# The couplings of a scan step moved into the last level of the step before

## The reference, cut to what matters

```python
def wkv_scan(r, w, k, v, a, b, S0, reverse):
    def step(S, inp):
        rt, wt, kt, vt, at, bt = inp
        sa = jnp.einsum('bhvk,bhk->bhv', S, at)
        S = S * wt[:, :, None, :] + sa[..., None] * bt[:, :, None, :] + vt[..., None] * kt[:, :, None, :]
        return S, jnp.einsum('bhvk,bhk->bhv', S, rt)
...
    for d in range(2):
...
        s_fin, yd = wkv_scan(rh, decay, kd, vh, -kk, kk * a, S0[d], reverse=(d == 1))
```

## Time and profile before

| | us |
|---|---|
| median of 3 runs | 2342.22 |
| lowest, highest | 2335.45, 2346.71 |
| the profiled execution | 2353.76 |
| its span, first to last instruction | 2352.0 |
| mean granted TensorE clock in it | 0.92 |
| first scan | 429 to 609 |
| second scan | 1611 to 1811 |

### The profile page before, as it was taken

One profiled execution on the slowest core, in us unless ns is written; L12 is line 12 of the kernel. 1 busy time (PEld: TensorE's weight loads), 2 busy tenths in 40 slices (PEclk: granted clock), 3 DMA queues, 4 the chain that ended last, 5 costly groups with the idle time before them and its releaser, 6 DMA issues. The chain is left out here.

```text
span 2352.0 us, 49452 instructions
## 1 busy us (share of the span) xinstructions
PE 2112.7 (90%) x21626; PEld 1341.5 (57%) x21626; DVE 682.5 (29%) x1672; ACT 540.6 (23%) x1260; POOL 266.3 (11%) x461
## 2 busy tenths in 40 slices
PE   6999999799899999999999599998998999987784
PEld 2454444688544444445556465556997787744442
DVE  1033334766331011210010214455465311200001
ACT  2123322455320001201111223323354301110011
POOL 0000000444000001101111200002333000011111
PEclk8999989889999999999999799996579999999897
DMA  7148717000122122539999711110000345799993
GB/s 286 69 155 345 294 37 253 3 4 4 55 90 107 54 92 96 223 111 390 397 397 389 275 37 51 61 50 2 3 3 8 151 149 190 271 382 400 393 403 118
DMA packets 55811, 399.64 MB, mean 170 GB/s; under 512 B 6672, under 2 KB 22928, under 8 KB 33648
## 3 DMA queue, kind: packets, MB, share of 16 engines
q1 hardware_dynamic: 43440, 361.94, 40.1%
q0 software_dynamic: 8576, 23.08, 2.6%
q10 hardware_dynamic: 3648, 12.45, 1.7%
HBM read 365.47 MB, written 31.98 MB: 169 GB/s over the span
## 5 line engine op out<-in xcount | busy, mean ns | idle before, releaser
L535 PE MATMUL ps<-H,memory 128*128 128x512 f32 (+2 forms) x1728 | 615.9, 513 | 8.8 <-DMA memory<-in_w_in 7.0
L535 PEld LDWEIGHTS ps<-H,memory 128*128 128x128 f32 (+1 forms) x1728 | 328.3, 191 | 284.9 <-issue 251.5
L1080 PE MATMUL ps<-memory 128*32 128x256 f32 x5120 | 302.1, 398 | 46.6 <-DMA memory<-in_eu 45.1
L535 PE MATMUL ps<-memory 128*128 128x512 f32 (+3 forms) x928 | 320.3, 496 | 6.7 <-issue 3.0
L1080 PEld LDWEIGHTS ps<-memory 128*32 128x32 f32 x5120 | 179.8, 115 | 164.9 <-issue 71.1
L535 PEld LDWEIGHTS ps<-memory 128*128 128x128 f32 (+1 forms) x928 | 173.9, 188 | 144.9 <-issue 127.5
L889 PE MATMUL ps<-memory 64*64 64x32 f32 x5120 | 223.1, 244 | 17.9 <-POOL memory L2042 6.9
L889 PEld LDWEIGHTS ps<-memory 64*64 64x64 f32 x5120 | 209.4, 164 | 28.5 <-POOL memory L2042 10.2
L1105 PE MATMUL ps<-memory 128*32 128x256 f32 x2560 | 144.8, 380 | 4.9 <-ACT memory L1468 3.8
L2042 POOL TENSOR_TENSOR memory<-memory,cons 128x256 f32<-128x256 f32 x160 | 113.2, 728 | 100.4 <-DVE memory L1725 78.8
L1105 PEld LDWEIGHTS ps<-memory 128*32 128x32 f32 x2560 | 80.0, 110 | 59.5 <-ACT memory L1468 10.1
(11 more groups left out here) (268 smaller groups left out, 2019.0 us busy)
## 6 DMA issues: line engine op xcount, KB each, us to landing
memory<-in_eg SPq DMA_DIRECT2D x32, 2048.0 KB, 16.6
memory<-in_eu SPq DMA_DIRECT2D x32, 2048.0 KB, 21.9
memory<-in_ed SPq DMA_DIRECT2D x32, 2048.0 KB, 22.8
memory<-in_w_ada SPq DMA_DIRECT2D x24, 2048.0 KB, 9.4
memory<-in_w_in SPq DMA_DIRECT2D x20, 2048.0 KB, 7.4
expert_rows<-memory SPq DMA_DIRECT2D x4, 3456.0 KB, 23.7
memory<-in_w_out SPq DMA_DIRECT2D x4, 2048.0 KB, 8.2
memory<-expert_rows ACTq DMA_DIRECT2D x19, 384.0 KB, 10.3
```

The source lines that it names most:

```text
L535: ins = mm(ps[0:M, bank, 0:w], lhs(k), rhs(k), start=(k == 0), stop=(k == n - 1))
L1080: ins = mm(out_.rearrange("p (x n) -> p x n", x=2), XGT[:, k, g * GROUP:g * GROUP + GROUP], sets[b][:, 0:2, k * 512 + c * P:k * 512 + c * ...
```

## The change

`couple(k + 1)` is issued in the last level of step k, between the join of side 1 and the two growths, instead of in step k + 1 between values and grams 1; `couple(0)` is issued ahead of the loop, before `grams(0, 0)`. A step then begins with grams 0, values, grams 1. The wait of the couplings for the last `inverse` of the step before becomes one for its first half level (`halved(N - 1, 1, d)`: the addition of level 0), which stands for the reading of the couplings' banks by VectorE. In the last level of the last step none is issued.

```diff
                     for d in both:
                         pe.wait_ge(sem("keys"), nth(N, d))
                         if N:
-                            pe.wait_ge(sem("inverse"), inverses(N - 1, 5, d))
+                            pe.wait_ge(sem("inverse"), halved(N - 1, 1, d))
...
+                couple(0)
                 for k in range(STEPS):
                     grams(k, 0)
                     if k:
                         values(k - 1)
-                    couple(k)
                     grams(k, 1)
                     for n in range(len(LEVELS)):
                         join(k, n, 0)
...
                         join(k, n, 1)
                         if k and n == 0:
                             correct_values(k - 1)
+                        if n == 4 and k + 1 < STEPS:
+                            couple(k + 1)
                         grow(k, n, 0)
                         grow(k, n, 1)
```

## The result

| | before | after |
|---|---|---|
| median, us | 2340.73 (10 runs, 2331.74 to 2352.43) | 2320.41 (10 runs, 2309.27 to 2328.78) |
| ratio, 95% interval | | 0.9905 (0.988 to 0.993) |
| the profiled execution, us (span) | 2353.76 (2352.0) | 2325.34 (2323.6) |

What follows compares the result with a forecast made beforehand. TensorE was taken to bound the scan at both clocks, leaving only its idle time to win: 4.3 + 1.7 + 0.4 + 0.7 - 0.4 - 0.65 - 0.85 = 5.2 us, so 2342.2 - 5.2 = 2337.0 us, range 2324 to 2352.

Steps and rivals of the forecast that it cites:

- The gaps: Scan: TensorE's idle time at step starts closes, 5.2 us less in sum; chance of this forecast 0.46.
- a wait before the couplings in both steps 0: Last level of step 0, each layer: couplings wait for VectorE's late keys, costing 0.65 and 0.85 us.
- A start at full clock: Step starts at full clock: first join's idle 0.46 to 0.41, second's 0.57 gone; 0.62 us each, seven starts, 4.3 us.
- A step at low clock: Four starts at low clock: no gap to close, gain 0; second layer's steps still 28.8 to 29 us.
- Starts behind two reads: Starts at 517 and 538, where grams 0 waits for GpSimd's queries: gain 0.84 each, 1.7 us for both.
- The beginning of the first scan: First layer: couplings run while grams 0 waits for GpSimd's queries; about 0.7 us won at the first join.
- The beginning of the second scan: Second layer: couplings want both keys where grams 0 waits for the first alone; 0.4 us lost.
- The clock: Low-clock spells inside steps: about 5.3 us each; forecast took spells as often as before, give or take one.
- rival 3: Step starts: the dense block loses the couplings, rises are missed at 11.4 us each; 2371.4 or 2359.8 us; chance 0.12.
- My own last sign of being wrong: Profile after: another number of low-clock steps, which would carry the result whatever the gaps did.
- Rival 2: Full-clock steps: less idle at starts prevents two clock falls, 10.6 us besides the 5.2; 2338.0 or 2326.4; chance 0.24.
- Rival 1: Step starts: ScalarE's later copies make the second join's gap reappear before the growth; about 2354 us; chance 0.18.

Runs made afterwards that it cites:

- e1: Changed kernel with the couplings issued behind the last level's two growths, directly ahead of grams 0: 2334.84 us, 0.997 of the kernel before.
- e3: Kernel before with the couplings moved early everywhere except in the second layer's four narrow steps: 2331.71 us, 0.9962 of the kernel before.
- e2: Kernel before with the couplings moved early only for the second layer's four narrow steps: 2332.88 us, 0.9956 of the kernel before.
- e9: Changed kernel with three extra one-column copies on ScalarE ahead of each step's values copies: 2317.37 us, run once.
- e10: Kernel before with three extra one-column copies on ScalarE ahead of each step's values copies: 2347.06 us, run once.
- e5: Changed kernel with the couplings of steps 2 and 3 of the second layer directly behind the update: 2318.56 us, 0.9908 of the kernel before.
- e6: The changed kernel itself, measured again with nothing altered: 2318.88 us, 0.991 of the kernel before.
- e4: Kernel before with only the couplings' wait weakened to the first half level, their place unchanged: 2338.04 us, 0.9986 of the kernel before.
- e8: Kernel before with the grams of the four narrow steps made full width, couplings at the old place: 2325.98 us, 0.9928 of the kernel before.

## Why the prediction was wrong, point by point

**The gaps (sum 5.2 us): right in mechanism, too small.** What I named came: the coupling matrix behind the last addition, the second join's wait gone, the first join waiting for ScalarE, the wait on the queries gone, a wait before the couplings in both steps 0 (0.65 and 0.85 us said, 0.7 and 0.84 found). The terms that were mis-sized:

- A start at full clock: 0.62 us said, 0.93 found. The first join's wait was to be 0.41 and is 0.58, since ScalarE starts its copies 0.27 us behind the start of grams 1, where I had 0.12. The gain I left out is larger: I took the 32 couplings at the same price in both places, and they cost 0.72 us between values and grams 1 and 0.38 in the last level. Seven starts: 2.2 us more than said.
- A step at low clock: unchanged, I said, 28.8 to 29. It is 28.4. The weight loads at such a start, after, answering to the earlier trace rows:

```profile
1653.51 1.78 PEld L805 LDWEIGHTS ps<-memory 64*128 64x128 f32 x16
1655.06 0.66 PEld L788 LDWEIGHTS ps<-cons,memory 64*128 64x128 f32 x8
1655.59 1.83 PEld L805 LDWEIGHTS ps<-memory 64*128 64x128 f32 x16
```

  From values to grams 1 it is 0.53 us here and was 1.83 in the step of the earlier trace rows (values at 1666.15, grams at 1667.98): 1.30 less, for 0.85 more between the last level's join of side 1 and grams 0.
- Starts behind two reads: 0.84 each said, 1.01 and 0.97 found (from the last level's join of side 1 to the first growth 7.71 and 7.62 us before, 6.70 and 6.65 after).
- The beginning of the first scan: 0.7 said, 0.8 found. From the end of the keys to the first join it was 5.74 us and is 4.92 (418.69 to 423.61). The second join of step 0, which waited 0.42 us, waits no more; I had left that out.
- The beginning of the second scan: 0.4 lost said, 0.24 found (from the end of the keys to the first join 4.68 us, now 4.92). With the wait before the couplings its step 0, at 0.50 in both traces, takes 0.7 us more (24.50 to 25.20).

By these the idle time comes to about 9 us: the 5.2, 2.2 for the starts, 0.4 for each of two low-clock steps and about 1 for the last three lines. The split over the runs gives 9.4, with e1 at 7.2 and e3 at 7.8. They agree as far as runs can tell.

**The clock: the step that failed.** My sum has no term for the clock. I let the number of spells vary by one or two inside full-clock steps, at 5.3 us each, and took the 123 us spell of the earlier trace rows as fixed, because TensorE was busy 99% in it and being busier could not end it. That being busy isn't enough stood in the rows; that nothing else could end the spell didn't follow. What I didn't ask is what TensorE was busy *with*. Where I weighed the couplings' new neighbours (rival 3), I counted what grams lose and took what readout and update gain as an offset, at a rise near 560 in the first scan, and never looked at the second layer, whose steps have narrow grams and no readout. There the update is the one block of products over all 128 partitions at a step's end (128*64 in its row, against 64*64 of a join), and the couplings now stand beside it. That carries about 12 of the 21 us. My own last sign of being wrong, another number of low-clock steps, is what came.

**Rival 2 (fewer spells, 2326.4 on the median's level, chance 0.24)** named the right kind and nearly the right size, at the wrong place and for the wrong reason. It had idle gaps at starts cause falls. e3 closes the gaps of every wide step and moves no low clock (342 against 340 us), and e1 closes them all and moves none. e2 leaves the wide steps as they were and moves 33 of the 44 us. So closed gaps aren't what raised the clock.

**Rival 1** fell: TensorE's waits on ScalarE's copies of the joins come to 3.0 us in the first scan, and were 2.9 before. In the second they rose from 2.6 to 4.4, since its narrow steps now run in part at full clock, where such waits show. In part it holds for the step itself: the wait of a start did change its name, from GpSimd's mask to ScalarE's values copies (e9, e10), but only one of the two came back.

**Rival 3** fell: rises came no later.

Hence the chances: 0.61 for no difference over 0.5% rested on rival 2's mechanism alone carrying the clock. The range was cut at 2324; the time was 2320.4. Even rival 2 with the 8 us of the gaps' upper bound in place of the 5.2 comes only to 2323.6 (2342.2 - 10.6 - 8). What was missing was a term for the long spell, of the 9.7 us that its four steps gave.

**What is shown, and what is argued.** Shown: the couplings' place beside the update or two growths behind it decides how much of the second scan runs at low clock (e1 against after), the four narrow steps carry it (e2, e3), it repeats (e5, e6, e9 against e4, e10), and wider grams at the old place do more (e8). Argued, and not shown: one common cause, that the clock goes by which products TensorE runs next to each other. For it speaks where the rises come: behind update, join and couplings in after, e2 and e6, behind wide grams, values and couplings in e8. Against a simple form of it speak the rises behind `solve` in after, e3 and e4, and that narrow grams, values and couplings in one row bring no rise, before or in e1.

The Trainium skill (TensorE: Matmul & The Clock Gate, section "Why this matters for your kernels") has continuous matmuls bring the full clock and gaps take it away. The first half doesn't hold here: a narrow step of before is busy 28.61 of 28.90 us and stays at 0.50, and the measurement decides. The second half isn't tested by these runs: the gaps that it warns of are much longer than the half microsecond at a start, so it gave rival 2 less support than the prediction says. Nor may the busy share of a step be set against its clock, as in 21.42 of 23.50 us at 0.78 in e8: that share is lower in part because the clock is higher.

Open: why the spells elsewhere in the program fall where they do. The profiled execution before has 36 us more at low clock than its kernel's mean (376 against 340); 21 us of that are the 41 against 20 in the first 400 us, and e2 and e3 have 41 there too, without a difference in their code.

## What to carry to other kernels

Look in the stretches for steps that stay at 0.50 with TensorE busy all the time: they need not be a floor, and the price was a third of their length here (28.8 us against 19.5). Try what stands next to what, and whether a narrow product can be made full width for nothing, before closing gaps of half a microsecond. When a reordering is costed, price each moved block at both places, with its neighbours, and give the clock its own term in the range, even where it has looked stuck.

## What the runs showed of the hardware that was not expected

- Widening the grams of four steps from 64 to 128 columns, half of it thrown away, took 15 us off the changed kernel (2318.9 to 2303.7) and 14 off the one before (2340.2 to 2326.0). It takes the four narrow steps from 111.2 to 92.2 us.
- 32 small matmuls cost 0.72 us in one place and 0.38 in another at the same clock, between values and grams and between a join and growths.
- Time at low clock costs 0.28 us per us over whole runs and 0.32 in a step of this scan ((28.8 - 19.5) / 28.8), not a half: much of a step isn't bound by TensorE's clock.
